# Attention stage of a four-layer kernel: scores issued three steps ahead, output copies one pair later, conditioning units and table load moved earlier

## What is computed

```python
# first block, layer 1: attention, three dilation groups, 8 heads of 64
qkv = (h @ w_qkv).reshape(B, S, 3, N_DIL_GROUPS, ATT_HEADS, HEAD_DIM)
logits = where(valid, q @ k.T * HEAD_DIM ** -0.5 + bias, NEG_INF)   # for each group and head
m = max(logits); p = exp(logits - m); den = sum(p); num = p @ v
o = sum_g(num_g * exp(m_g - m_all)) / sum_g(den_g * exp(m_g - m_all))
y = o @ w_out
# second block: conditioning, used only after the first block
mod = (silu(c) @ ada_w[i] + ada_b[i])          # 1024 x 9216 weights for each of two layers
```

## Time and profile before

| what | us |
|---|---|
| median of the runs shown (3) | 1584.15 |
| lowest, highest | 1583.92, 1585.43 |
| the profiled execution | 1589.87 |
| its span | 1588.1 |
| TensorE busy | 1502.1 (95%) |
| VectorE busy | 1050.7 (66%) |
| ScalarE busy | 704.5 (44%) |
| mean granted clock | 0.979 |

### The profile page before, as it was taken

How to read it: one execution, slowest core, us unless ns; L and a number is a source line. 1 busy time by engine, 2 the same in 40 slices (tenths; PEclk the granted TensorE clock), 3 DMA queues, 4 the chain that set the end, 5 groups by cost and what they waited for, 6 DMA issues and landing times.

```text
span 1588.1 us, 17185 instructions
## 1 busy us (share of the span) xinstructions
PE 1502.1 (95%) x6957; PEld 1226.2 (77%) x6957; DVE 1050.7 (66%) x1222; ACT 704.5 (44%) x881; POOL 39.1 (2%) x63
## 2 busy tenths in 40 slices
PE   6999999999589999899998899998999999999998
PEld 4778888888467888678887688886788878778886
DVE  5658767655549666677886778886644564764554
ACT  5345444543445444534343533435334453453442
POOL 1000000000000000100000000000000000000000
PEclk9999999999899999999999899999999999999999
DMA  7449778558418788568995279895455545455552
GB/s 260 159 134 329 273 263 289 172 183 277 121 55 302 261 291 302 202 214 296 318 323 199 80 258 320 302 317 194 159 185 186 186 159 186 141 177 186 186 187 91
DMA packets 202267, 346.19 MB, mean 218 GB/s; under 512 B 9627, under 2 KB 105123, under 8 KB 202188
## 3 DMA queue, kind: packets, MB, share of 16 engines
q1 hardware_dynamic: 164172, 269.58, 51.0%
q10 hardware_dynamic: 38016, 75.50, 13.1%
HBM read 343.96 MB, written 1.09 MB: 217 GB/s over the span
## 4 chain that ended last, share of the span: by engine, by line
PE 84%; DVE 7%; ACT 3%; issue 2%; DMA 2%; POOL 1%; SPq 0%; DVEq 0%; POOLq 0%; ACTq 0%
PE up_ps L1324 51%; PE acc L1324 28%; PE tr_ps L1419 3%; DVE w_lo L866 1%; DMA ada_raw<-in_ada_w 1%; DVE ada_acc L939 1%; ACT w_hi L527 1%; POOL msq L499 1%; DVE res L978 1%; ACT xn L547 1%; PE tr_ps L1609 1%; DVE xn L975 1%; PE tr_ps L1506 1%; POOL rstd L493 1%; DVE xn L882 0%
## 5 line engine op out<-in xcount | busy, mean ns | idle before, releaser
L866 DVE TENSOR_TENSOR w_lo<-raw,w_hi 128x2048 fp32r<-128x2048 f32 x245 | 555.1, 2287 | 182.3 <-ACT w_hi L527 182.2
L1324 PE MATMUL up_ps<-w_hi,xT_hi 128*128 128x512 f32 x1264 | 505.0, 399 | 8.2 <-DVE xT_lo L896 7.1
L1324 PE MATMUL up_ps<-w_hi,xT_lo 128*128 128x512 f32 x1264 | 496.4, 393 | 0.0
L1324 PE MATMUL up_ps<-w_lo,xT_hi 128*128 128x512 f32 x1264 | 495.5, 392 | 0.0
L527 ACT ACTIVATE w_hi<-raw 128x2048 fp32r<-128x2048 f32 x245 | 459.9, 1915 | 27.5 <-DMA raw<-in_conv_w_in 11.6
L1324 PEld LDWEIGHTS up_ps<-w_hi,xT_hi 128*128 128x128 f32 x1264 | 239.8, 190 | 61.9 <-issue 6.9
L1324 PEld LDWEIGHTS up_ps<-w_hi,xT_lo 128*128 128x128 f32 x1264 | 239.2, 189 | 51.6
L1324 PEld LDWEIGHTS up_ps<-w_lo,xT_hi 128*128 128x128 f32 x1264 | 240.2, 190 | 47.3
L1324 PE MATMUL acc<-w_hi,hT_hi 128*128 128x512 f32 x624 | 199.6, 394 | 0.0
L939 DVE SCALAR_TENSOR_TENSOR ada_acc<-ada_raw,cond,ada_acc 128x512 f32<-128x512 f32 x252 | 189.2, 751 | 14.7 <-DMA ada_raw<-in_ada_w 7.0
L1324 PE MATMUL acc<-w_hi,hT_lo 128*128 128x512 f32 x624 | 197.8, 391 | 0.0
(11 more groups left out here) (125 smaller groups left out, 833.2 us busy)
## 6 DMA issues: line engine op xcount, KB each, us to landing
raw<-in_ffn_w_in SPq DMA_DIRECT2D x176, 512.0 KB, 4.9
ada_raw<-in_ada_w ACTq DMA_DIRECT2D x72, 1024.0 KB, 7.6
raw<-in_ffn_w_out SPq DMA_DIRECT2D x88, 512.0 KB, 4.6
raw<-in_w_up SPq DMA_DIRECT2D x64, 512.0 KB, 5.6
raw<-in_w_down SPq DMA_DIRECT2D x64, 512.0 KB, 4.4
raw<-in_b_w_qkv SPq DMA_DIRECT2D x36, 512.0 KB, 4.5
raw<-in_conv_w_in SPq DMA_DIRECT2D x24, 512.0 KB, 4.4
raw<-in_a_w_in SPq DMA_DIRECT2D x16, 512.0 KB, 7.3
```

Source lines behind the costliest of these rows:

```text
L866: nc.vector.tensor_tensor(w_lo[:, slot, :], raw[:, slot, :], w_hi[:, slot, :].bitcast(F32), ALU.subtract).then_inc(lo_ready, 1)
L1324: return nc.tensor.matmul(dst, a, b, start=start, stop=stop, skip_group_check=True)
```

## The change

It has four parts. (1) The conditioning units 8 and 9: their loads move on ScalarE's queue from the v chunks to the starts of q/k chunks c = 0 (both halves of unit 8), 2 and 3; their multiply-adds on VectorE move to the ends of chunks c = 1 to 4. (2) ScalarE does an exponential of one column in v chunk b = 2, whose result is overwritten later. (3) TensorE issues `scores` three steps ahead in place of two. (4) `out_hi` and `out_lo` of a pair come later on their engines: `out_hi` behind items 8 and 12 and behind `copy_probs(14)`, `out_lo` behind items 9 and 13 and, for pair 2, behind the stage's last weight split.

```diff
@@ ScalarE, q and k chunks
             for c in range(6):
                 g = p.slab + 2 * c
+                for u, s in (((0, 0), (0, 1)), (), ((1, 0),), ((1, 1),), (), ())[c]:
+                    load_ada(ADA_AT["qkv"] + u, s)
                 ahead(g)
@@ ScalarE, v chunks
-                if b < 2:
-                    load_ada(ADA_AT["qkv"] + b, 0)
                 ahead(g)
+                if b == 2:
+                    nc.scalar.activation(den[:, 0:1], neg_half[:, 0:1], ACT.Exp)
...
                 if b < 2:
-                    load_ada(ADA_AT["qkv"] + b, 1)
                     ahead(g + 1)
@@ ScalarE, attention
                 if i >= 2:
                     copy_probs(i - 2)
-                if i > 4 and i % 4 == 3:
-                    out_hi(i // 4 - 1)
+                if i >= 8 and i % 4 == 0:
+                    out_hi(i // 4 - 2)
...
             copy_probs(ITEMS - 2)
+            out_hi(PAIRS - 2)
             copy_probs(ITEMS - 1)
             out_hi(PAIRS - 1)
@@ VectorE, q and k chunks, v chunks
                 ahead(g + 1)
+                if 1 <= c <= 4:
+                    ada(ADA_AT["qkv"] + (c - 1) // 2, (c - 1) % 2)
...
                 if b < 2:
-                    ada(ADA_AT["qkv"] + b, 0)
                     ahead(g + 1)
-                    ada(ADA_AT["qkv"] + b, 1)
@@ VectorE, attention
                 normalise(i)
-                if i > 4 and i % 4 == 3:
-                    out_lo(i // 4 - 1)
+                if i >= 8 and i % 4 == 1:
+                    out_lo(i // 4 - 2)
             ahead(at["attn"].slab - 1)
-            out_lo(PAIRS - 1)
+            for pair in range(PAIRS - 2, PAIRS):
+                out_lo(pair)
@@ TensorE, attention
-            scores(0)
-            scores(1)
+            for s in range(3):
+                scores(s)
             for i in range(ITEMS):
                 turn_probs(i)
-                if i % 2 and i // 2 + 2 < 2 * PAIRS:
-                    scores(i // 2 + 2)
+                if i % 2 and i // 2 + 3 < 2 * PAIRS:
+                    scores(i // 2 + 3)
```

## The result

| | before | changed |
|---|---|---|
| median, us | 1584.79 (4 runs) | 1564.67 (4 runs) |
| lowest to highest, us | 1583.92 to 1586.45 | 1563.99 to 1564.84 |
| the profiled execution, us | 1589.87 | 1563.99 |
| first scores to first matmul of the output projection, us | 57.76 | 36.53 |
| mean granted clock in that stretch | 0.82 | 0.91 |

The ratio of the runs is 0.9865, 95% interval 0.985 to 0.988: 20.1 us less by the medians. The forecast was 18.0 us less (1566.1), in a range from 1561.5 to 1576.

What follows compares the result with a forecast made beforehand. No engine is full in the attention stage; waits between engines, at the entry and in a ring in the loop, bound it. 21.6 us (entry included) less 3.0 clock less 0.6 tight links gives 18.0 us: 1566.1, range 1561.5 to 1576.

Steps and rivals of the forecast that it cites:

- Entry: Start of the attention stage: first transposes at 403.55 instead of 406.55, 3.0 us gained by early units and table load.
- Loop: Attention loop: scores three ahead and later output copies bring attends 7 to 9 us apart, before 11.4.
- What is late next: Before the transposes of item 12: weight split and output copy on ScalarE leave TensorE idle 2.8 us.
- Clock: Attention stage: half clock near the third attend and at the start costs 3.0 us, bounds 0 and 11.
- 0.6 us for tight links: Attention stage: 0.6 us taken off the gain for links that the sum took as tight.
- q and k chunks at no cost: q and k chunks: moved units cost 0, bounds 0 to 5 us; ScalarE's load wait doesn't reach TensorE.
- Bias rows: Attention stage: third pair's DMA issued at 404.4, landing 3.5 to 5.5 us later, 409.9 at worst, needed at 410.09.
- A: Rival, attention stage: clock stays half, gain 11 us, range 8 to 14.5, time 1573; chance 0.20.
- B: Rival: only the entry gives, the loop's ring isn't opened; gain 3 to 6 us, time 1580; chance 0.06.
- C: Rival: nothing measurable, waits in the q and k chunks eat the entry gain, loop gives nothing; chance 0.03.
- D: Rival, q and k chunks: slower, as shared DMA engines starve TensorE; 17 us net loss, 1601; chance 0.05.
- the main ring: Attention loop: transposes, exponentials and scores wait for each other, 11.4 us from one attend to the next.

Runs made afterwards that it cites:

- e1: Kernel before with only the conditioning units moved and the table loaded early; stage 54.46 us, ratio 0.9981, median 1585.21 us.
- e7: Changed kernel without the early one-column exponential, so the table loads before the first real one; stage 36.86 us, ratio 0.9874, median 1565.61 us.
- e4: Changed kernel with conditioning units and table load back in their old places; stage 40.44 us, ratio 0.9874, median 1568.43 us.
- e2: Kernel before with only the scores issued three steps ahead; stage 44.73 us, ratio 0.9891, median 1571.25 us.
- e5: Changed kernel with the output copies back in their old places; stage 40.71 us, ratio 0.9894, median 1568.64 us.
- e8: Changed kernel with the stage's weight split moved later on ScalarE and VectorE; stage 33.09 us, ratio 0.9839, median 1560.79 us.
- e11: Changed kernel with 10 unread filler matmuls behind the transposes of item 11; stage 36.51 us, ratio 0.9858, median 1564.27 us.
- e6: Changed kernel with the scores two steps ahead again; stage 54.18 us, ratio 0.9966, median 1581.43 us.
- e9: Changed kernel with 24 unread filler matmuls behind the transposes of item 11; stage 38.67 us, ratio 0.9877, median 1565.97 us.
- e12: Changed kernel measured again, word for word; stage 36.47 us, ratio 0.9866, median 1565.58 us.

## Why the prediction was right

By its own steps, as times behind the first scores (forecast: minus 399.66):

| step | forecast | measured | before |
|---|---|---|---|
| first transposes | 3.89 | 3.83 | 6.86 |
| first attend | 13.64 | 13.23 | 24.26 |
| second attend | 20.99 | 20.31 | 37.74 |
| third attend | 30.24 | 29.53 | 49.12 |
| fourth attend's output copy | 36.3 | 36.65 | 57.88 |
| output projection, full clock | 36.19 | 36.53, partly at half clock | 57.76 |

- **Entry, 3.0 us.** Right: 3.03 in the changed kernel, 3.30 of the stage in e1. The table's share is smaller than it seems from the 1.29 us on ScalarE: 0.50, e7. The sum had that in it without saying so, as it let the logits of item 2 decide. The forecast set 0.6 us aside for half clock at the start; it stayed full, which the traces show only together with the lead (e4).
- **Loop.** Right, step by step, within 0.7 us. The leading cause is the lead of the scores (13.0 us alone, e2); the later copies are 4.2 us on top (e5) and work as the forecast's order of queues says. The remark that ScalarE would be the busiest engine was wrong: from the first attend to the second TensorE is busy 7.08 of 7.08 us, ScalarE 5.59.
- **What is late next.** Right, and shown by e8: the split moved away takes 3.4 us off the stage. Forecast idle 2.8 us, measured 2.54.
- **Clock, 3.0 us.** The mechanism and the place were right, the size too large. The forecast had 1.9 at the third attend, 0.5 behind it and 0.6 at the start. Measured: 1.3 at the third attend (3.51 in place of 2.2), nothing at the start. Of the rest, the transposes at half clock lie beside the exponentials and normalising, which were the later ones anyway: in e11 the transposes of items 12 and 13 ran at full clock, and the third attend came only 0.1 us sooner.
- **0.6 us for tight links.** Not needed; the links were pessimistic by 0.7 us up to the third attend. This and the clock are the 3 us between the stage's 21.2 and the forecast's 18.0. The medians, at 20.1, are 2.1 from the forecast, 1.1 nearer than the stage, and for that no cause is known, so it is luck; executions of before spread over 9 us across the study (1583.6 to 1592.5), and what that does to the median of four runs wasn't pursued. The range's upper end was put at 22.6 us gained with no clock loss, where the sum has 21.6; with the split moved and the clock full, e8 gained 24.7 in the stage.
- **q and k chunks at no cost.** Right for TensorE. ScalarE's wait is there, twice and longer than the bound: the forecast spoke of one load behind VectorE's unit and at most 5 us; both later loads wait. ScalarE's timeline of the changed kernel in the chunks:

```profile
319.49 1.92 ACT L527 ACTIVATE w_hi<-raw 128x2048 fp32r<-128x2048 f32 x1 [5.54 <-DVE ada_acc L941]
321.31 0.58 ACT L692 ACTIVATE xn<-up_ps 128x512 f32<-128x512 f32 x1
323.32 0.60 ACT L692 ACTIVATE xn<-up_ps 128x512 f32<-128x512 f32 x1 [1.44 <-PE up_ps L1327]
...
332.24 1.92 ACT L527 ACTIVATE w_hi<-raw 128x2048 fp32r<-128x2048 f32 x1 [6.52 <-DVE ada_acc L941]
334.06 0.58 ACT L692 ACTIVATE mid<-up_ps 128x512 f32<-128x512 f32 x1
336.72 0.60 ACT L692 ACTIVATE mid<-up_ps 128x512 f32<-128x512 f32 x1 [2.08 <-PE up_ps L1327]
```

  The step that failed is the bound on that wait: it counted the unit and the split, not the time in which VectorE's queue hadn't come to the unit. In the trace of before, whose chunks lie 4.38 us later, the first copies of the third and fourth chunk stand at 325.00 and 338.41: so they lost 0.69 us (321.31) and 0.03 us (334.06). ScalarE's idle time ahead of each chunk's second copy took that up, it is still 1.44 and 2.08 us, and TensorE's wait in the third chunk is 0.44 us in both traces. The weight splits that were late had three slabs of lead to cover them. The cost of 0 was right with some 1.4 us to spare, not with the margin that the forecast gave. Its sum for VectorE, 35.5 us busy, put all four half units into the window; two lie in it, and 28.90 was measured.
- **Bias rows.** Right: the first was issued 4.67 us behind the first scores (forecast 4.7), they landed 3.3 to 5.4 us later (5.5 at worst), and VectorE waited for no DMA in the stage.
- **The rivals.** A (half clock throughout) was wrong: 0.91. B (only the entry gives) is what the stage would be without the lead of the scores: e6 has 3.6 us. C (nothing) is out by the interval and by e2. D never came near: the chunks took 268 GB/s beside a full TensorE, and 401 GB/s were moved at 410 to 413 in the stage, so its 328 GB/s of room was too low an estimate.

## What to carry to other kernels

Where no engine is full, follow one round of the loop and ask which instruction stands ahead of what the others need: here one more step of lead for the producer gave 13 of 21 us, and copies that wait for a long matmul belong behind everything that doesn't. Side work in such a stage goes where its engine waits anyway: the same 1.9 us split cost 3.4 us at one place and nothing at another. Small parts are worth more once the main ring is open, so measure them on top of it, and compare by the stage's own length when the runs spread wider than the effect.

## What was not expected of the hardware

The granted clock makes small gaps dear or free. A late start of 2.55 us became 4.33 at the first attend (e4), where TensorE, busy 0.94 of 3 us, then had 1.2 instead of 2.4 GHz. That such a stretch costs this much is seen in e9 as well: with the start of the changed kernel to 0.01 us, its first attend came 1.6 us later once the clock had fallen. Filling the 2.5 us gap with 2.40 us of matmuls did not keep the clock up (e11), while 5.52 us did (e9, one trace) and taking the stall away did too (e8, 1.00). Identical code had the half clock at the same place in two profiled executions (e12) and at another in a third, ahead of the only difference (e9). The Trainium skill (TensorE: Matmul & The Clock Gate, HAM oscillation) advises, for thin matmuls that wait for DMA, to restructure the loop so that TensorE stays warm, that is at full clock. The waits here are for ScalarE and VectorE, but e8, a matter of order alone, agrees: 3.4 us less with the clock at 1.00.
